# Norm entries of a two-block transformer kernel: queue order on three engines, two queues for x, the mean folded into the root, six half chunks rounded inside the norm

## The reference, cut to what matters

```python
def rmsnorm(x, g):
    xf = x.astype(jnp.float32)
    y = xf * lax.rsqrt(jnp.mean(xf * xf, axis=-1, keepdims=True) + EPS)
    return (y * g.astype(jnp.float32)).astype(x.dtype)

# first block
h = rmsnorm(x, attn_norm_g)
z = h @ w_in                                  # entry "in1"
x = x + jnp.concatenate([y_pool, y_attn], axis=-1) @ w_out      # "out1"
x = x + conv_ffn(rmsnorm(x, ffn_norm_g), w_up, conv_w, conv_b, w_down)   # entry "up1", then "down1"
# second block: the norm has a scale and a shift from c_act @ w_mod
h = rmsnorm_2(x, mix_pre_w[l]) * (1 + sc_m) + sh_m
y = hybrid_mixer(h, w_in[l], ...)             # entry "in2", then "out2"
x = x + g_m * rmsnorm_2(y, mix_post_w[l])
h = rmsnorm_2(x, ffn_pre_w[l]) * (1 + sc_f) + sh_f
y = conv_ffn_2(h, w_up[l], ffn_conv_w[l], w_down[l])             # entry "up2", then "down2"
x = x + g_f * rmsnorm_2(y, ffn_post_w[l])
```

## Time and profile before

| | |
|---|---|
| time, median of 3 runs | 2273.74 us (2272.29 to 2276.62) |
| profiled execution, its own time | 2274.06 us |
| its span in the trace | 2271.8 us |
| PE busy | 2239.2 us, 99% of the span |
| DVE busy | 1605.6 us, 71% |
| ACT busy | 1143.4 us, 50% |
| POOL busy | 73.0 us, 3% |
| DMA | 515.06 MB, mean 227 GB/s |

### The profile page before, as it was taken

The page is one execution under the profiler, slowest core; times in us unless marked ns, Lnnn a source line. Parts: engine busy times, 40 slices in busy tenths (PEclk is TensorE's granted clock), DMA queues, the critical chain, the costliest instruction groups (busy, mean ns, idle before and its releaser), DMA issues.

```text
span 2271.8 us, 32854 instructions
## 1 busy us (share of the span) xinstructions
PE 2239.2 (99%) x12498; PEld 1958.1 (86%) x12498; DVE 1605.6 (71%) x1894; ACT 1143.4 (50%) x1417; POOL 73.0 (3%) x48
## 2 busy tenths in 40 slices
PE   8999999999999999999999999999999999999998
PEld 7879888888888888888798999878888888888887
DVE  5579677788888767767755676777888666665555
ACT  5454545555455554444535454555455554544444
POOL 0005200000000000000000110000000000000000
PEclk9999999999999999999999999999999999999999
DMA  8657376687878766778475455766878655555553
GB/s 310 221 168 260 130 259 234 235 287 281 285 275 289 258 191 229 305 269 313 160 257 185 149 167 167 246 216 204 291 276 284 204 189 193 191 185 195 193 189 125
DMA packets 195717, 515.06 MB, mean 227 GB/s; under 512 B 16457, under 2 KB 18457, under 8 KB 171689
## 3 DMA queue, kind: packets, MB, share of 16 engines
q1 hardware_dynamic: 191033, 511.51, 65.0%
q10 hardware_dynamic: 4592, 2.25, 0.3%
HBM read 511.61 MB, written 2.11 MB: 226 GB/s over the span
## 4 chain that ended last, share of the span: by engine, by line
PE 94%; DVE 3%; ACT 1%; issue 0%; DMA 0%; POOL 0%; SPq 0%; DVEq 0%; ACTq 0%
PE ps L1750 28%; PE ps L1707 16%; PE ps L1708 16%; PE ps L1709 16%; PE ps L1759 15%; DVE w_lo L991 1%; PE ps L2087 1%; PE ps L1907 0%; ACT w_hi L501 0%; DVE x L1601 0%; DVE region L1247 0%; DMA x<-in_x 0%; ACT region L547 0%; DVE region L1089 0%; PE ps L1995 0%
## 5 line engine op out<-in xcount | busy, mean ns | idle before, releaser
L991 DVE TENSOR_TENSOR w_lo<-raw,w_hi 128x1024 fp32r<-128x1024 f32 x768 | 953.9, 1251 | 602.0 <-ACT w_hi L501 601.4
L501 ACT ACTIVATE w_hi<-raw 128x1024 fp32r<-128x1024 f32 x768 | 810.2, 1059 | 929.2 <-PE ps L1709 502.5
L1750 PE MATMUL ps<-a_hl,w_hi 128*128 128x512 f32 x2816 | 673.3, 391 | 3.4 <-DVE a_hl L1081 1.9
L1750 PEld LDWEIGHTS ps<-a_hl,w_hi 128*128 128x128 f32 x2816 | 517.6, 188 | 103.4 <-issue 3.8
L1707 PE MATMUL ps<-w_hi,a_hl 128*128 128x512 f32 x1248 | 488.8, 392 | 2.2 <-DVE a_hl L1115 2.2
L1708 PE MATMUL ps<-w_lo,a_hl 128*128 128x512 f32 x1248 | 486.4, 390 | 0.0
L1709 PE MATMUL ps<-w_hi,a_hl 128*128 128x512 f32 x1248 | 486.3, 390 | 0.0
L1759 PEld LDWEIGHTS ps<-a_hl,w_lo 128*128 128x128 f32 x2816 | 362.4, 192 | 13.8
L1759 PE MATMUL ps<-a_hl,w_lo 128*128 128x256 f32 x2816 | 366.6, 284 | 0.0
L1707 PEld LDWEIGHTS ps<-w_hi,a_hl 128*128 128x128 f32 x1248 | 234.4, 188 | 53.0 <-issue 4.5
L1709 PEld LDWEIGHTS ps<-w_hi,a_hl 128*128 128x128 f32 x1248 | 234.4, 188 | 49.0
(11 more groups left out here) (183 smaller groups left out, 891.1 us busy)
## 6 DMA issues: line engine op xcount, KB each, us to landing
raw<-in_w_up SPq DMA_DIRECT2D x176, 1024.0 KB, 5.1
raw<-in_w_mod SPq DMA_DIRECT2D x96, 1024.0 KB, 5.2
raw<-in_w_in SPq DMA_DIRECT2D x88, 1024.0 KB, 5.1
raw<-in_w_down SPq DMA_DIRECT2D x88, 1024.0 KB, 4.9
raw<-in_w_out SPq DMA_DIRECT2D x32, 1024.0 KB, 5.3
x<-in_x SPq DMA_DIRECT2D x4, 512.0 KB, 5.8
region<-gate_rows ACTq DMA_DIRECT2D x2, 1024.0 KB, 8.0
out_x<-x SPq DMA_DIRECT2D x8, 256.0 KB, 2.2
```

The costliest lines, as they stand in the source:

```text
L501: nc.scalar.activation(w_hi[:, hh % HL_SLOTS, :], raw[:, n % RAW_SLOTS, half * HALF:(half + 1) * HALF], ACT.Copy).then_inc(hi_ready, 1)
L991: v.tensor_tensor(w_lo[:, hh % HL_SLOTS, :], raw[:, n % RAW_SLOTS, half * HALF:(half + 1) * HALF], w_hi[:, hh % HL_SLOTS, :].bitcast(F32), ...
L1750: mm = mmul(dst[:, BLOCK * ft:BLOCK * (ft + 1)], w_hi[:, hh % HL_SLOTS, columns(kk, ft)], a_hl[:, kt, :, :].rearrange("p l s -> p (l s)"), ...
```

## The change

It has eight pieces.

1. `mean_square` and `post_mean` leave out the multiplication and the addition of epsilon; the root takes the sum with a scale of 1/D and epsilon as a bias (`deviation`, `post_deviation`). A constant column `EPS_AT` is set at the start, and a first root of it comes ahead of the work.
2. x: the first halves of both token tiles stay on SyncE's queue, the second halves go to ScalarE's, ahead of the constants and `attn_norm_g`. The first weight chunk is loaded as two halves.
3. TensorE: the late transposes are divided. k = 4 and 5 come after chunk 0, k = 6 and 7 after chunk 1.
4. TensorE: `keep_busy` counts and places are other ones: in1 4, 2, 3 in place of 2, 0, 3; up1 2 and 3 in place of 3 and 0; in2 3 and 3 in place of 4 and 0; up2 11 and 3 in place of 11 and 0.
5. Weight halves h4 and h5 are rounded inside the norm of in1 and in2 too; h1's rest in up1 goes from before the last part of x into the norm, behind lows(1), and in in2 and up2 from behind lows(0) to behind lows(1).
6. In in2 and up2 the first pair is handed over one feature tile at a time (`first_hi`, one more signal of `xt_ready`).
7. In in2 and up2 VectorE's second quarter of tile 1 comes behind evict(1), and in up2 the second half of tile 0 as well.
8. In in1 ScalarE rounds h0 between its two parts of the norm.

```diff
+        EPS_AT = 287
...
             def load_columns(n, src):
+                if n == 0:
+                    dst = raw[:, 0, :].rearrange("p (k n) -> p k n", k=KC)
+                    src = src.rearrange("(k p) n -> p k n", p=P)
+                    sp.dma_start(dst[:, 0:2, :], src[:, 0:2, :]).then_inc(sem("first_half"), 16)
+                    sp.dma_start(dst[:, 2:4, :], src[:, 2:4, :]).then_inc(raw_full[0], 16)
+                    return
...
             for t in range(TT):
-                for half in range(2):
-                    cols = slice(D // 2 * half, D // 2 * (half + 1))
-                    sp.dma_start(x[:, t, cols], x_in[t * P:(t + 1) * P, cols]).then_inc(sem(f"x_loaded{t}{half}"), 16)
+                sp.dma_start(x[:, t, 0:D // 2], x_in[t * P:(t + 1) * P, 0:D // 2]).then_inc(sem(f"x_loaded{t}0"), 16)
...
             def deviation(p, t):
-                act.wait_ge(sem("ms_ready"), 2 * p + t + 1)
-                nc.scalar.activation(sm(SD + 2 * p + t), sm(MS + 2 * p + t), ACT.Sqrt).then_inc(sem("sd_ready"), 1)
+                act.wait_ge(sem("ss_ready"), 2 * p + t + 1)
+                nc.scalar.activation(sm(SD + 2 * p + t), sm(SS + 2 * p + t), ACT.Sqrt, bias=sm(EPS_AT), scale=1.0 / D).then_inc(sem("sd_ready"), 1)
...
-            def norm(p, name, halves, scale=None):
+            def norm(p, name, halves, scale=None, behind=None):
                 normed_part(p, 1)
+                if behind:
+                    behind()
                 normed_part(p, 3)
                 for k in range(KT // 2):
-                    if scale is None:
-                        act.wait_ge(sem("xt_ready"), 8 * (p - 2) + k + 1)
+                    if scale is None and k == 0:
+                        for kk in range(2):
+                            act.wait_ge(sem("xt_ready"), 9 * (p - 2) + kk + 1)
+                            ins = nc.scalar.activation(a_hi[:, kk, :], xt[:, kk, :], ACT.Copy)
+                            if kk == 0:
+                                ins.then_inc(sem("first_hi"), 1)
...
+            for t in range(TT):
+                act.dma_start(x[:, t, D // 2:], x_in[t * P:(t + 1) * P, D // 2:]).then_inc(sem(f"x_loaded{t}1"), 16)
             loads = [(con[:, 0:C_LVL], consts[:, 0:C_LVL]),
...
+            act.wait_ge(sem("eps_set"), 1)
+            nc.scalar.activation(sm(SD + 8), sm(EPS_AT), ACT.Sqrt)
...
-            lead("in1", range(1))
-            norm(0, "in1", {0: (1,), 2: (2,), 4: (3,)}, colA(A_ATTN, KT))
+            norm(0, "in1", {0: (1,), 2: (2,), 4: (3,), 5: (4,), 6: (5,)}, colA(A_ATTN, KT), lambda: lead("in1", range(1)))
...
-            norm(2, "in2", {0: (1,), 2: (2,), 4: (3,)})
+            norm(2, "in2", {0: (1,), 2: (2,), 4: (3,), 5: (4,), 6: (5,)})
...
             def mean_square(p, t, n=4):
                 dve.wait_ge(sem(f"sq{p}{t}"), n)
-                link(v.tensor_reduce(sm(SS + 2 * p + t), sm(N_SS + 8 * p + 4 * t, n), AX_X, ALU.add))
-                v.tensor_scalar(sm(MS + 2 * p + t), sm(SS + 2 * p + t), 1.0 / D, EPS, ALU.mult, ALU.add).then_inc(sem("ms_ready"), 1)
+                v.tensor_reduce(sm(SS + 2 * p + t), sm(N_SS + 8 * p + 4 * t, n), AX_X, ALU.add).then_inc(sem("ss_ready"), 1)
...
                 def lows(k):
+                    if shift is not None and k == 0:
+                        dve.wait_ge(sem("first_hi"), p - 1)
+                        v.tensor_tensor(a_lo[:, 0, :], xt[:, 0, :], a_hi[:, 0, :].bitcast(F32), ALU.subtract)
+                        dve.wait_ge(act_hi, 8 * f + 1)
+                        v.tensor_tensor(a_lo[:, 1, :], xt[:, 1, :], a_hi[:, 1, :].bitcast(F32), ALU.subtract).then_inc(act_ready, 1)
+                        return
...
-                normed_block(p, 2)
+                if shift is None:
+                    normed_block(p, 2)
                 if p == 0:
-                    normed(0, 0, HALVES[1])
+                    normed(p, 0, HALVES[1])
                     lead(name, (0,))
                 for k in range(KT // 2):
                     if shift is not None and k + 1 < KT // 2 and k > 0:
                         evict(k + 1)
                     lows(k)
                     if shift is not None and k == 0:
                         evict(1)
+                        normed_block(p, 2)
+                        if p == 3:
+                            normed(p, 0, HALVES[1])
                     for h in halves.get(k, ()):
                         lead(name, (h,))
...
-            norm(0, "in1", {1: (1,), 3: (2,), 5: (3,)}, colA(A_ATTN, KT))
+            norm(0, "in1", {1: (1,), 3: (2,), 5: (3,), 6: (4,), 7: (5,)}, colA(A_ATTN, KT))
...
             normed(1, 0, HALVES[0])
-            lead("up1", range(1, 2))
...
-            norm(1, "up1", {2: (2,), 3: (3,), 5: (4,), 7: (5,)}, colA(A_FFN, KT))
+            norm(1, "up1", {1: (1,), 2: (2,), 3: (3,), 5: (4,), 7: (5,)}, colA(A_FFN, KT))
...
-            norm(2, "in2", {0: (1,), 2: (2,), 4: (3,)}, sm(SCALE_M, KT), modc[:, 0:KT])
+            norm(2, "in2", {1: (1,), 2: (2,), 4: (3,), 6: (4,), 7: (5,)}, sm(SCALE_M, KT), modc[:, 0:KT])
...
-            for half in range(2):
-                normed(3, 0, HALVES[half])
+            normed(3, 0, HALVES[0])
             mean_square(3, 1)
-            norm(3, "up2", {0: (1,), 2: (2,), 3: (3,), 5: (4,), 7: (5,)}, sm(SCALE_F, KT), modc[:, 48:64])
+            norm(3, "up2", {1: (1,), 2: (2,), 3: (3,), 5: (4,), 7: (5,)}, sm(SCALE_F, KT), modc[:, 48:64])
...
+            keep_busy(4)
+            turn(0, 0, range(4))
             keep_busy(2)
-            turn(0, 0, range(4))
             turn(0, 1, range(4))
             keep_busy(3)
...
             def mixer1(at):
-                if at == 0:
-                    for k in range(4, 8):
+                if at < 2:
+                    for k in (4 + 2 * at, 5 + 2 * at):
                         turn(0, 0, (k,))
                         turn(0, 1, (k,))
...
             turn(1, 0, range(4))
+            keep_busy(2)
+            turn(1, 1, range(4))
             keep_busy(3)
-            turn(1, 1, range(4))
...
             turn(2, 0, range(4))
-            keep_busy(4)
+            keep_busy(3)
             turn(2, 1, range(4))
+            keep_busy(3)
...
             turn(3, 1, range(4))
+            keep_busy(3)
```

More of the change, by code:

```diff
@@ L496, in round_half @@
                 n, hh = RAW_OF[m], 2 * m + half
-                if half == 0:
+                if hh == 0:
+                    act.wait_ge(sem("first_half"), 16)
+                elif half == 0 or hh == 1:
                     act.wait_ge(raw_full[n % RAW_SLOTS], 16 * (n // RAW_SLOTS + 1) + r * raw_add)
@@ L523, in body @@
                     for c in range(8):
-                        if i0 > 0 or c >= 2:
+                        if i0 > 0 or c >= (3 if name in ("in1", "in2") else 2):
                             for half in range(2):
@@ L686, in load_table @@
             def load_table(n):
-                nc.scalar.activation(sm(SPARE + n), ones[:, 0:1], ACT.Sqrt)
+                nc.scalar.activation(sm(SPARE + n - 1), ones[:, 0:1], ACT.Sqrt)
             def first_columns():
@@ L1090, in evict @@
                                               shift[:, kt:kt + 1], ALU.mult, ALU.add)
+                        if k == 0 and kk == 0:
+                            ins.then_inc(sem("xt_ready"), 1)
                     ins.then_inc(sem("xt_ready"), 1)
@@ L1895, in turn @@
                     if t == 0:
-                        pe.wait_ge(sem("hn_dve"), 4 * p + (4 if p == 0 and k > 3 else k // 4 + 1))
+                        pe.wait_ge(sem("hn_dve"), 4 * p + (4 if p in (0, 3) and k > 3 else k // 4 + 1))
                         if turned_there(p, k) >= 0:
@@ L1903, in turn @@
                     else:
[L1904 removed]
+                        pe.wait_ge(sem("hn_dve"), 4 * p + (2 if p in (0, 3) else 3) + k // 4)
                     for kk in range(2):
```

18 lines of the change are left out of this document (10 added, 8 removed).

## The result

The changed kernel takes 2284.62 us in the median of 5 runs (2283.82 to 2287.31), against 2273.74 before (2272.29 to 2276.62). The ratio is 1.005, 95% interval 1.0035 to 1.0065: slower by 10.9 us, where 10.8 had been forecast (2284.5). The profiled execution is the slowest of the five, 2287.31 us with a span of 2285.0, so its trace holds 13.2 us more than the trace of before.

A forecast was written before the change was run, and what follows sets the result against it. TensorE, busy 99% of the span, was taken to bound the kernel. Entries and end summed to +8.0, clock +2.9, so +10.9; 2274.06 + 10.9 - 0.3 = 2284.7, stated as 2284.5 us, range 2276.5 to 2289.5.

The forecast's parts named there:

- in1, first real matmul: Start of in1: small loads wait behind x until about 10.1, first real matmul at 18.9 instead of 17.08, +1.8 us.
- in1, chunk 2, beyond that: Chunk 2 of in1: the rest of h4 stands behind lows(6) on VectorE, so TensorE waits; net +3.6 us.
- up1: Entry up1: h5 waits for work behind the late transposes and starts at 394.8 instead of 394.0, net +0.8 us.
- in2: Entry in2: chunk 2 starts at 1134.6 instead of 1133.19, +1.4 us with every earlier gain inside it.
- up2, to h5: Entry up2: h5 starts at 1549.8 instead of 1549.2, +0.6 us, all gains spent.
- the end: Kernel's end, where VectorE is on the last chain: folding the mean saves once more, -0.2 us.
- new falls of the clock, in1 and up2: Behind the new waits in in1 and up2: two new drops to the low clock, 1.45 us each, +2.9 (bounds 0 and 5.8).
- Folding the mean into the root: Norm chains at up1, in2, up2 and the end: one VectorE step and its semaphore leave, about 0.2 us each.
- Rival D: All four entries: late transposes hidden, VectorE finishing the rests of h4 and h5 during chunk 1; -9.7, 2264 us, chance 8%.
- Rival A: Start of in1 and clock: small loads are not late and the clock holds; +5.7, 2279.5 us, chance 17%.
- C: A wash: in1's start gains 0.5, VectorE's shorter steps recover about 1 us at each of four waits; 2275.5 us, chance 11%.
- Rival B: Clock falls at all four entries and once more in in1; +13.8, 2287.5 us, chance 14%.

## Why the prediction was right

Point by point, by its own steps; "measured" is the trace of the changed kernel against that of before.

| step | predicted, us | measured, us |
|---|---|---|
| in1, first real matmul | +1.8 | +1.98 |
| in1, chunk 2, beyond that | +3.6 | +3.47 (36.69 against 31.24) |
| up1 | +0.8 | +1.07 |
| in2 | +1.4 | +1.46 |
| up2, to h5 | +0.6 | +0.94 |
| the end | -0.2 | -0.25 |
| new falls of the clock, in1 and up2 | +2.9 | +1.65 and +2.88 |
| sum | +10.9 | +13.2 |

The idle stretches were predicted at 2.6, 1.5, 3.9 and 2.5 us and are 2.54, 1.51, 3.89 and 2.31. The walk through each queue, piece by piece with the durations of the trace before, was good to 0.35 us a step, because the pieces did not change their durations: a lower half took 1250 ns on average after as against 1251 before. The two numbers on the clock are what is left of the differences when the starts are taken off, not durations of their own.

**The start of in1** was an estimate: small loads at 10.1, measured 10.0. x itself came 0.6 us earlier than before (its last part released VectorE at 8.69 instead of 9.27), not at the same time, but TensorE was still busy with its filling matmuls. That the first real matmul came at 19.06, with 18.9 forecast, is in part luck. Three more kernels ran with the same start, and their small load released TensorE at 9.93 to 10.02 too; their first real matmuls came at 18.99, 17.66 and 17.43, the last two outside the forecast's 18.0 to 19.7. What differs is when TensorE comes to full pace: 16.3 and 16.1 us in the two late ones, 13.5 and 13.0 in the early ones. With the start of before it came at 17.08, 17.20 and 16.57. So the direction and the cause hold, and the size is 1.3 us by the means of the two groups, with 0.2 and 2.5 as the outermost pairs. The Trainium skill ("DMA: Bandwidth & Descriptors", "Queues, rings and completion order"), by which one queue's descriptors are taken in order, agrees with the small load's row. In the kernel with the small loads first the two queues did not share evenly: SyncE's first 1 MB was there at 6.7 us, when ScalarE went on with it, and of ScalarE's queue the first 0.64 MB only at 9.35.

**The clock** was right in the price of one fall, 1.45 us, where the filled waits show 1.49 and 1.46. It was off in what a fall can be and in where it comes. In the profiled execution the low stretch of up2 lasted 6.8 us instead of 3.4, which is the +2.88 in the table. And "1.9 and more brought a fall, 1.47 none" is no rule: the clock fell after 1.48 us in two kernels and held after 3.43 in one. The two falls forecast as new did come in this trace; in the kernel with the small loads first the one in in1 did not, behind the same 2.54 us. Against the median (+10.9) the sum came out exact, which is luck: +8.7 for the waits and the start leave about 2.2 for the clock, a remainder and not a measurement. Of the 2.7 us between this execution and the median the longer low stretch can explain some 1.3, and the start or one more fall the other 1.4, since each differed by that much between the traces; no trace of a median execution exists. The Trainium skill ("TensorE: Matmul & The Clock Gate", "HAM oscillation") describes a kernel whose waits of 3 to 5 us bring the clock down each time anew. Three of the four waits here were shorter than those, so it bore less on this term than the prediction took from it, when it saw the term nearer to 5.8; up1's wait of 1.51 brought no fall here, and 3.43 us brought none in the kernel with the division alone.

**Folding the mean into the root** was put at 0.2 us a chain. The root with its bias and scale takes 0.29 us on ScalarE where the plain one took 0.20, so a part of the gain goes there. That part is read from rows; no run isolates it.

**Rival D** had named its own condition: the rest of h4 ahead of evict(6) in VectorE's queue. With exactly that edit the kernel took 2268.6 us. D's price was 2264, and the two kernels with still more rests ahead went to 2265.0 and 2262.0. What D had priced at nothing or too low are waits that its condition leaves: 1.34 us for h3 in in1, 1.03 for h3 in in2, 1.59 for h1 in up2. So the prediction held on the order of a few instructions in a queue, and the forecast would have been wrong by 16 us with them exchanged. Rival A failed on both its conditions, since the small load was late and the clock fell; C failed because the steps kept their durations. Rival B's time, 2287.5, is that of the slowest run (2287.31), but not by B's way: it counted a fall in up1 and a second one in in1 that weren't there.

Open: what decides whether an idle stretch of about 1.5 or 2.5 us brings the clock down, and when TensorE comes to full pace at the start; and what each of the small parts of the change (mean, halves of the first pair, the second half of tile 0 in up2) is worth alone. Together with `keep_busy` they give 4.1 us; `keep_busy` alone gave about 1, within the noise.

## What to carry to other kernels

When work on the limiting engine is put off, look in the helper engine's queue for what stands behind the pieces that now come late: independent work there is late too, and that, not the moved work, sets the price. Put the independent pieces ahead of the dependent ones before moving anything. A gain at one entry is not lost at the waits behind it if the engine that sets them starts earlier too: lay two traces over each other and follow the distance, since medians that differ by the clock's falls can hide a term of 1.7 us. A small load behind large ones on the same queue waits for them, 3.7 us here.
